# In the last group ScalarE shares the key search, and kept keys are marked behind it

## The chip, the cores and the metric

The kernel runs on one core of a Trainium2 chip. The metric is device time in microseconds (us) of one execution, lower is better. Engines: TensorE (PE, its weight loads PEld), VectorE (DVE), ScalarE (ACT), GpSimd (POOL) and SyncE (SP), which issues most DMAs.

## The reference

One decoder block on x of 2048 rows by 1024. A projection of the normed x gives a convolution branch, queries of 8 heads, one shared key and value head of 64, an indexer (8 small heads) and gates. For each row the indexer scores all earlier keys; the 256 highest are kept, and attention with ALiBi runs over the kept keys only. Then come the gated sum, a projection, a SwiGLU FFN of width 2816, and norms.

```python
rel = jax.nn.relu(jnp.einsum('bqhd,bsd->bqhs', qib, k_idx))
score = jnp.einsum('bqh,bqhs->bqs', wb, rel).astype(jnp.float32)
score = jnp.where(causal[None], score, -jnp.inf)
_, idx = lax.top_k(score, topk)          # topk = 256
...
x = x + merged @ w_out[layer]
hf = _rmsnorm(x, norm_ffn[layer])
x = x + (jax.nn.silu(hf @ w_ffn_gate[layer]) * (hf @ w_ffn_up[layer])) @ w_ffn_down[layer]
```

## The kernel before, in words

The rows are worked in four groups (g = 0 to 3) of 512, each of four row tiles of 128 (t = 0 to 3). The work has three kinds of stage: A (projection, convolution, gates, and at its end the indexer's scores), C (attention and output projection) and F (FFN). Their order is A0 C0, A1 F0 C1, A2 F1 C2, A3 F2 C3, F3: the FFN of a group runs behind the next group's A. Each engine has its own program, written out by hand in this order; semaphores tie them together.

*Key search* (L1143 to L1200, DVE, in stage A's program, but in time under the next F). SC holds each row's scores in f32, (4g + t + 1) * 128 of them for tile t; in group 3 these are 1664, 1792, 1920 and 2048. The search finds the 256th highest score bit by bit: in each of 31 turns of a loop (`one_bit`, L1165) DVE counts for each tile the scores at or above a candidate (L1151), then sets or leaves the bit (L1175 `change`, L1178 `cand`). A last count gives `room`, how many ties at the threshold may be kept (L1194).

*Marks* (`mark`, L948). For each unit of up to 512 keys four steps on DVE mark what is kept: L968 ties, L970 running rank of ties, L975 rank within room, L978 mark into SC (and a copy of the carry, L973). POOL turns marks into the mask M of distances (L505, L509). For groups 1 and 2 `marks_ahead` has tiles one to three (counted from 0) marked right behind the search; for groups 0 and 3 they are marked inside C, one unit in each of the first iterations of a row tile, between DVE's attention steps (L1226 to L1276): 12 units of up to 512 keys in C3. Tile 0 is always marked and masked by `first_mask` (L988), which DVE runs near the end of F.

*Stage F* (PE L1578 on, ACT L851 on, POOL L518 on). The 22 slices of the FFN's width go in parts of 8, 8 and 6. For each slice j of a part PE does a gate chunk into bank 6 and an up chunk into bank 7 (24 matmuls each); ACT applies Silu to the first (L873), copies the second (L878), POOL multiplies (L526), ACT and POOL split the product into high and low part (L864, L531). Then follow n row chunks (the down projection). PE may begin gate chunk j + 1 when Silu j is done, up chunk j + 1 when copy j is done. POOL adds earlier parts into XR (L539), and behind the last part's second down chunk writes the distances (`distances`, L472), which wait for `topk_done`, that is `room`. DVE's first mask waits for all additions to XR and for the distances.

*Border F to C.* DVE adds the last part into NY (L1327, four times); behind each of these ACT issues a DMA of two heads' queries (L907), and PE's first scores (L1555) wait for these.

*Stage C.* 16 pairs of heads (4 tiles x 4). For each head: PE scores in two parts, DVE adds the mask and takes the running minimum (L1251), ACT Exp (L809), PE transposes, ACT and DVE split them (L796, L1259), PE multiplies with the values; once per pair DVE takes a reciprocal (L1273).

The lines that set the order around the change:

```python
def marks_ahead(g):
    return 0 < g < GROUPS - 1
...
dve.wait_ge(y_added, 2 * RT * (len(PARTS) - 1) * (g + 1))
if g + 1 < GROUPS:
    first_mask(g + 1)
```

Of the kernel before, what the change touches and what calls it, by code (L numbers as in the profile page):

```python
# [23 lines left out]
def build_block(nc, A):  # L24
# [71 lines left out]
    def units(b):  # L96

        n = (b + 1) * P
        return [(s, min(512, n - s)) for s in range(0, n, 512)]

    IDX_UNITS = [sum(HEADS * len(units(b)) for b in blocks(g) if picks(b)) for g in range(GROUPS)]
    PICKED = [sum(picks(b) for b in blocks(g)) for g in range(GROUPS)]

# [17 lines left out]
    with ctx:  # L121
# [100 lines left out]
        idx_psum, idx_relu, idx_sum = sem("idx_psum"), sem("idx_relu"), sem("idx_sum")  # L222
        bit_step, topk_done, dist_ready = sem("bit_step"), sem("topk_done"), sem("dist_ready")
        mark_step, marked0, marked, m0_ready, m_ready, s_psum, s_masked, exp_done = sem("mark_step"), sem("first_keys_marked"), sem("keys_marked"), sem("first_mask_ready"), sem("mask_ready"), sem("s_psum"), sem("scores_masked"), sem("exp_done")
        pt_psum, pt_hi, pt_ready, pt_used = sem("pt_psum"), sem("pt_hi"), sem("pt_ready"), sem("pt_used")
# [88 lines left out]

        MASK_BASE = [sum((RT - 1) * (a + 1) for a in range(g)) for g in range(GROUPS)]

# [271 lines left out]
        def _(act):  # L588
# [53 lines left out]
            for ph, g in ORDER:  # L642
# [208 lines left out]
                else:  # L851
# [5 lines left out]
                    if g < GROUPS - 1:  # L857
                        act.wait_ge(idx_sum, sum(IDX_UNITS[:g + 2]))
                    for n in PARTS:
                        base_h = h_done  # L860
# [6 lines left out]
                        for j in range(n):  # L867
                            s = j % 2
                            used(c0 + 2 * j)
                            hi(c0 + 2 * j + 2, 0)  # L870
                            if j >= 2:
                                act.wait_ge(h_ready, base_h + j - 1)
                            nc.scalar.activation(TMP[:, s, :], PS[:, 6, :], ACT.Silu).then_inc(sg_done, 1)  # L873
                            if j >= 1:
                                h_hi_part(j - 1)
                            used(c0 + 2 * j + 1)
                            hi(c0 + 2 * j + 3, 1)
                            nc.scalar.activation(TMP[:, 2 + s, :], PS[:, 7, :], ACT.Copy).then_inc(up_done, 1)  # L878
                        c0 += 2 * n
                        h_done += n  # L880
                        for j in range(n - 1):
                            used(c0 + j)
                            hi(c0 + j + 2, (c0 + j) % 2)
                            if j == 0:
                                h_hi_part(n - 1)
                        if last_part:
                            hi(c0 + n + 1, 1)
# [27 lines left out]
        def _(dve):  # L915
# [32 lines left out]
            def mark(t, b, u, step):  # L948
# [33 lines left out]
                marks[0] += 1  # L982

            def marks_ahead(g):

                return 0 < g < GROUPS - 1

# [44 lines left out]
            for ph, g in ORDER:  # L1032
                c0 = BASE[ph, g]
                if ph == "A":
# [81 lines left out]
                    for t, b in enumerate(blocks(g)):  # L1116
# [23 lines left out]
                        dve.wait_ge(idx_sum, idx_done)  # L1140
                        chained(nc.vector.tensor_tensor(out=SC[:, t, n - P:n], in0=SC[:, t, n - P:n], in1=upper[:, :], op=ALU.add))


# [17 lines left out]
                    chained(nc.vector.tensor_scalar(flip[:, :], count[:, :], float(TOPK), -1.0, ALU.is_lt, ALU.mult))  # L1161
                    chained(nc.vector.tensor_tensor(out=cand[:, :], in0=trial[:, 0:1].to_broadcast([P, RT]), in1=flip[:, :], op=ALU.bitwise_xor))
                    TURNS = len(chosen) + 2

# [16 lines left out]

                    if g == 0:

# [4 lines left out]
                    else:  # L1188
                        with dve.Fori(0, 31) as i:
                            one_bit(i)  # L1190
                    turns[0] += 30 * TURNS

                    count_rows(ALU.is_gt, chained)
# [437 lines left out]
```

## Time and profile before

| | us |
|---|---|
| median of 3 runs | 3488.89 (3484.62 to 3489.68) |
| the profiled execution | 3484.34 |
| its span, first to last instruction | 3482.5 |
| PE busy | 3214.0 (92%) |
| DVE busy | 2176.4 (62%) |
| ACT busy | 1183.2 (34%) |
| POOL busy | 715.5 (21%) |
| mean granted TensorE clock, share of full speed | 0.975 |

The sums of the prediction are made on the profiled execution; its span leaves out 1.8 us around the instructions. Busy shares are means over stages with different limits, so the stages are read one by one. A timeline row gives start, duration, engine, line, operation, output <- inputs, count, and in brackets the engine's idle time before it and what ended that.

### The profile page before, as it was taken

Reading aid. Unit: us, or ns where it says so; the run is one execution under the profiler, and the core shown is the slowest. Engines: PE = TensorE matmul, PEld = TensorE weight load, DVE = VectorE, ACT = ScalarE, POOL = GpSimd, SP = SyncE. Lnnn points to the kernel's source line nnn. Section 1 sums busy time; section 2 is a strip of 40 time slices with the busy share of each in tenths; the row PEclk is TensorE's granted clock in tenths of the full one; section 3 lists DMA queues with packets and bytes.
Section 4 is the critical chain, followed back from the end, with each engine's and each line's share of the span. In section 5 each row is a group of like instructions: output and inputs, shape, how many; then the busy total and the mean of one; then the engine's idle time right before and its main releaser. Section 6 shows DMA issues by size and latency. Waiting matters only on the chain.

```text
span 3482.5 us, 41585 instructions
## 1 busy us (share of the span) xinstructions
PE 3214.0 (92%) x15045; PEld 2623.4 (75%) x15045; DVE 2176.4 (62%) x3647; ACT 1183.2 (34%) x2028; POOL 715.5 (21%) x482
## 2 busy tenths in 40 slices
PE   7991799999999999999999889999999968889998
PEld 6871688778887888768887778875888756768886
DVE  2758727588824827599894872759999988710001
ACT  3341541253335631261112753127111156521111
POOL 3430110035767000001214200000221231001212
PEclk9995899999999999999999999999999999999999
DMA  7970565569996366535555125652555510255554
GB/s 229 301 243 0 182 254 206 188 230 290 289 291 227 134 229 207 180 145 193 193 193 181 67 96 222 207 184 99 194 194 193 189 49 22 108 196 193 193 193 165
DMA packets 177613, 640.14 MB, mean 184 GB/s; under 512 B 11341, under 2 KB 95353, under 8 KB 115608
## 3 DMA queue, kind: packets, MB, share of 16 engines
q1 hardware_dynamic: 160800, 575.71, 48.0%
q10 hardware_dynamic: 16632, 61.96, 4.6%
q8 instruction: 121, 1.98, 0.2%
q14 instruction: 60, 0.49, 0.0%
HBM read 476.14 MB, written 161.48 MB: 183 GB/s over the span
## 4 chain that ended last, share of the span: by engine, by line
PE 64%; DVE 15%; issue 12%; ACT 5%; DMA 2%; POOL 1%; DVEq 0%; ACTq 0%; SPq 0%; POOLq 0%
PE PS L1391 14%; PE PS L1362 13%; PE PS L1364 13%; PE PS L1363 13%; DVE flags L1151 2%; PE PS L1510 2%; DVE probs L1251 2%; DVE W L1136 1%; PE PS L1376 1%; PE PS L1377 1%; PE PS L1378 1%; DMA RAW<-in_w_in 1%; ACT probs L809 1%; DVE PT L1259 1%; PE PS L1345 1%
## 5 line engine op out<-in xcount | busy, mean ns | idle before, releaser
L1151 DVE TENSOR_SCALAR_CACHE_REDUCE flags<-W,cand 128x1408 uint8<-128x1408 f32 (+3 forms) x462 | 683.5, 1479 | 53.8 <-DVE cand L1178 40.0
L1391 PE MATMUL PS<-WS,HT 128*128 128x512 f32 x2088 | 483.4, 391 | 5.1 <-POOL WS L455 2.8
L1391 PEld LDWEIGHTS PS<-WS,HT 128*128 128x128 f32 x2088 | 394.0, 189 | 88.5 <-issue 3.6
L526 POOL TENSOR_TENSOR TMP<-TMP 128x512 f32<-128x512 f32 x88 | 114.8, 1304 | 1538.8 <-ACT TMP L878 1538.8
L1362 PE MATMUL PS<-HF,WS 128*128 128x512 f32 x1072 | 417.4, 389 | 4.4 <-DVE HF L942 2.5
L1364 PE MATMUL PS<-HF,WS 128*128 128x512 f32 x1072 | 417.1, 389 | 0.0
L1363 PE MATMUL PS<-HF,WS 128*128 128x512 f32 x1072 | 417.1, 389 | 0.0
L455 POOL TENSOR_TENSOR WS<-RAW,WS 128x1024 fp32r<-128x1024 f32 x116 | 279.5, 2410 | 609.7 <-ACT WS L598 566.3
L1362 PE MATMUL PS<-HT,WS 128*128 128x512 f32 x824 | 325.2, 395 | 1.2 <-POOL WS L455 1.2
L1364 PE MATMUL PS<-HT,WS 128*128 128x512 f32 x824 | 320.8, 389 | 0.0
L1363 PE MATMUL PS<-HT,WS 128*128 128x512 f32 x824 | 320.6, 389 | 0.0
L1327 DVE TENSOR_TENSOR attn<-PS,XR 128x1024 f32<-128x1024 f32 x16 | 18.9, 1219 | 365.6 <-PE PS L1391 365.4
L1510 PE MATMUL PS<-ident,probs 128*128 128x128 f32 x1088 | 178.4, 286 | 70.9 <-ACT probs L809 28.6
L1362 PEld LDWEIGHTS PS<-HF,WS 128*128 128x128 f32 x1072 | 201.2, 188 | 47.5 <-issue 3.1
L598 ACT ACTIVATE WS<-RAW 128x1024 fp32r<-128x1024 f32 x114 | 120.8, 1059 | 335.3 <-PE PS L1364 151.5
L1364 PEld LDWEIGHTS PS<-HF,WS 128*128 128x128 f32 x1072 | 201.2, 188 | 41.7
L1363 PEld LDWEIGHTS PS<-HF,WS 128*128 128x128 f32 x1072 | 201.2, 188 | 41.7
L1016 DVE SCALAR_TENSOR_TENSOR PS<-W,cw,PS 128x512 f32<-128x512 f32 x336 | 221.9, 744 | 0.0
L1555 PE MATMUL PS<-KH,QS 128*128 128x512 f32 (+3 forms) x320 | 129.5, 405 | 99.8 <-DVE mx L1251 70.8
L1510 PEld LDWEIGHTS PS<-ident,probs 128*128 128x128 f32 x1088 | 128.6, 146 | 109.7 <-issue 60.7
L1391 PE MATMUL PS<-W,HT 128*128 128x512 f32 x792 | 184.9, 389 | 0.0
L1362 PEld LDWEIGHTS PS<-HT,WS 128*128 128x128 f32 x824 | 154.7, 188 | 35.6 <-issue 4.0
(219 smaller groups left out, 6039.0 us busy)
## 6 DMA issues: line engine op xcount, KB each, us to landing
WS<-split_weights_scratch SPq DMA_DIRECT2D x234, 1024.0 KB, 4.8
split_weights_scratch<-WS SPq DMA_DIRECT2D x116, 1024.0 KB, 5.0
W<-split_weights_scratch SPq DMA_DIRECT2D x114, 1024.0 KB, 4.8
RAW<-in_w_in SPq DMA_DIRECT2D x34, 512.0 KB, 6.1
RAW<-in_w_ffn_gate SPq DMA_DIRECT2D x22, 512.0 KB, 6.3
RAW<-in_w_ffn_up SPq DMA_DIRECT2D x22, 512.0 KB, 6.3
RAW<-in_w_ffn_down SPq DMA_DIRECT2D x22, 512.0 KB, 5.7
gate_b_scratch<-TMP ACTq DMA_DIRECT2D x32, 256.0 KB, 5.2
```

What stands on the lines that cost most here:

```text
L455: nc.gpsimd.tensor_tensor(out=WS[:, slot, 1, :], in0=RAW[:, slot, :], in1=WS[:, slot, 0, :].bitcast(f32), op=ALU.subtract).then_inc(w_lo, 1)
L526: nc.gpsimd.tensor_tensor(out=TMP[:, s, :], in0=TMP[:, s, :], in1=TMP[:, 2 + s, :], op=ALU.mult).then_inc(h_prod, 1)
L598: nc.scalar.activation(WS[:, slot, 0, :], RAW[:, slot, :], ACT.Copy).then_inc(w_hi, 1)
L1016: nc.vector.scalar_tensor_tensor(out=TAPSUM[:, c, :], in0=GLU[:, c, ds(k0 + i, ROWS)], scalar=cw[:, c, ds(k0 + i, 1)], in1=TAPSUM[:, c, :] ...
L1151: step(nc.vector.tensor_scalar(flags[:, 0:n], SC[:, t, 0:n], cand[:, t:t + 1].bitcast(f32), 0.0, op, ALU.add, accum_out=count[:, t:t + 1]))
L1251: nc.vector.tensor_tensor_reduce(out=prob(g, i, e)[:, s:s + w], in0=score_bank(r)[:, 0:w], in1=M[:, b % RT % 2, s:s + w].bitcast(f32), sca ...
L1362: mm(PS[:, bank, :], wh, src[:, 0, k, :], start=k == 0, stop=False)
L1363: mm(PS[:, bank, :], wh, src[:, 1, k, :], start=False, stop=False)
L1364: ins = mm(PS[:, bank, :], wl, src[:, 0, k, :], start=False, stop=k == KD - 1)
L1391: ins = mm(PS[:, 2 * t + half, :], lhs, split(c, w_part)[:, half * 512:(half + 1) * 512], start=first and part == 0 and w_part == 0, stop= ...
L1510: ins = nc.tensor.transpose(PS[:, 4 + k % 2, (2 * a + e) * P:(2 * a + e + 1) * P], prob(g, i, e)[:, (k0 + a) * P:(k0 + a + 1) * P], ident[ ...
L1555: mm(o, lhs, KH[:, s:s + w], start=True, stop=False)
```

## The change

Only group 3 is touched (`split_counts`). Its search loop runs on two engines: in each of the 31 turns DVE counts tiles 0 and 1 over 1792 scores (below the candidate), ACT tiles 2 and 3 over 2048 scores as a sum of signs of candidate minus score. The shorter rows are filled up to these lengths with the masked value. DVE waits for ACT's two sums, takes the bit step for all four tiles at once and posts the next trial. ACT's turns stand in F2's program: one behind each Silu (and high part) and one behind each up copy, none ahead of the first up copy, and one in each down chunk but the last two of a part; they stop at 31. ACT writes its signs into IH and IL, which nothing reads by then. A sum of signs can't tell ties at the candidate exactly, so `raise_by_one` behind the loop tries the next higher number for tiles 2 and 3. And `marks_ahead` now holds for group 3 too: the marks of row tiles two to four (t = 1 to 3) stand behind the search and no longer in C3.

```diff
--- before.py
+++ after.py
@@ -99,6 +99,11 @@
         return [(s, min(512, n - s)) for s in range(0, n, 512)]
 
     IDX_UNITS = [sum(HEADS * len(units(b)) for b in blocks(g) if picks(b)) for g in range(GROUPS)]
+    BITS = 31
+    SPLIT = RT // 2
+    COUNT_DVE, COUNT_ACT = SEQ - TOPK, SEQ
+
+
     PICKED = [sum(picks(b) for b in blocks(g)) for g in range(GROUPS)]
 
 
@@ -221,6 +226,7 @@
         qs_out, qs_in = sem("qs_out"), [sem(f"qs_in{t}") for t in range(RT)]
         idx_psum, idx_relu, idx_sum = sem("idx_psum"), sem("idx_relu"), sem("idx_sum")
         bit_step, topk_done, dist_ready = sem("bit_step"), sem("topk_done"), sem("dist_ready")
+        trial_ready, act_counted = sem("trial_ready"), sem("rows_counted_by_act")
         mark_step, marked0, marked, m0_ready, m_ready, s_psum, s_masked, exp_done = sem("mark_step"), sem("first_keys_marked"), sem("keys_marked"), sem("first_mask_ready"), sem("mask_ready"), sem("s_psum"), sem("scores_masked"), sem("exp_done")
         pt_psum, pt_hi, pt_ready, pt_used = sem("pt_psum"), sem("pt_hi"), sem("pt_ready"), sem("pt_used")
         rsb_ready, recip_done, pv_psum, bc_done, att_done = sem("rsb_ready"), sem("recip_done"), sem("pv_psum"), sem("bc_copied"), sem("att_done")
@@ -312,7 +318,7 @@
             return W3[:, part, :] if SLOT[c] == 2 else WS[:, SLOT[c], part, :]
 
 
-        MASK_BASE = [sum((RT - 1) * (a + 1) for a in range(g)) for g in range(GROUPS)]
+        MASK_BASE = [sum((RT - 1) * (a + 1) for a in range(g)) for g in range(GROUPS + 1)]
 
         def att_j(j):
             return att[:, j, 0:ROWS]
@@ -856,6 +862,19 @@
                     act.dma_start(XR[:, :, :], x1_dram[g]).then_inc(x1_in, 16)
                     if g < GROUPS - 1:
                         act.wait_ge(idx_sum, sum(IDX_UNITS[:g + 2]))
+                    turn = 0
+
+                    def count_rows():
+
+                        nonlocal turn
+                        if g + 2 != GROUPS or turn == BITS:
+                            return
+                        act.wait_ge(trial_ready, turn + 1)
+                        for t, seen in ((SPLIT, IH), (SPLIT + 1, IL)):
+                            nc.scalar.activation(seen[:, 0:COUNT_ACT], SC[:, t, 0:COUNT_ACT], ACT.Sign, scale=-1.0,
+                                                 bias=cand[:, t:t + 1].bitcast(f32), accum_out=count[:, t:t + 1]).then_inc(act_counted, 1)
+                        turn += 1
+
                     for n in PARTS:
                         base_h = h_done
 
@@ -873,9 +892,13 @@
                             nc.scalar.activation(TMP[:, s, :], PS[:, 6, :], ACT.Silu).then_inc(sg_done, 1)
                             if j >= 1:
                                 h_hi_part(j - 1)
+                            if j >= 1 or c0 > BASE[ph, g]:
+                                count_rows()
                             used(c0 + 2 * j + 1)
                             hi(c0 + 2 * j + 3, 1)
                             nc.scalar.activation(TMP[:, 2 + s, :], PS[:, 7, :], ACT.Copy).then_inc(up_done, 1)
+                            if j < n - 1:
+                                count_rows()
                         c0 += 2 * n
                         h_done += n
                         for j in range(n - 1):
@@ -883,6 +906,8 @@
                             hi(c0 + j + 2, (c0 + j) % 2)
                             if j == 0:
                                 h_hi_part(n - 1)
+                            if j < n - 2:
+                                count_rows()
                         if last_part:
                             hi(c0 + n + 1, 1)
                         if not last_part:
@@ -981,9 +1006,13 @@
                 ins.then_inc(mark_step, 1)
                 marks[0] += 1
 
+            def split_counts(g):
+
+                return g + 1 == GROUPS
+
             def marks_ahead(g):
 
-                return 0 < g < GROUPS - 1
+                return g > 0
 
             def first_mask(g):
 
@@ -1139,6 +1168,10 @@
                                 idx_done += 1
                         dve.wait_ge(idx_sum, idx_done)
                         chained(nc.vector.tensor_tensor(out=SC[:, t, n - P:n], in0=SC[:, t, n - P:n], in1=upper[:, :], op=ALU.add))
+                        if split_counts(g):
+                            to = COUNT_DVE if t < SPLIT else COUNT_ACT
+                            if n < to:
+                                chained(nc.vector.memset(SC[:, t, n:to], MASKED))
 
 
 
@@ -1159,8 +1192,13 @@
                     chained(nc.vector.memset(cand[:, :], 0))
                     count_rows(ALU.is_ge, chained)
                     chained(nc.vector.tensor_scalar(flip[:, :], count[:, :], float(TOPK), -1.0, ALU.is_lt, ALU.mult))
-                    chained(nc.vector.tensor_tensor(out=cand[:, :], in0=trial[:, 0:1].to_broadcast([P, RT]), in1=flip[:, :], op=ALU.bitwise_xor))
-                    TURNS = len(chosen) + 2
+                    ins = nc.vector.tensor_tensor(out=cand[:, :], in0=trial[:, 0:1].to_broadcast([P, RT]), in1=flip[:, :], op=ALU.bitwise_xor)
+                    if split_counts(g):
+                        ins.then_inc(trial_ready, 1)
+                        dve.wait_ge(trial_ready, 1)
+                    else:
+                        chained(ins)
+                    TURNS = 3 if split_counts(g) else len(chosen) + 2
 
                     def one_bit(i):
 
@@ -1179,7 +1217,52 @@
                                                             scalar=trial[:, ds(i + 1, 1)],
                                                             in1=cand[:, :], op0=ALU.bitwise_xor, op1=ALU.bitwise_xor))
 
-                    if g == 0:
+                    def one_bit_split(i):
+
+                        def turn(ins):
+
+                            ins.then_inc(bit_step, 1)
+                            turns[0] += 1
+                            dve.wait_ge(bit_step, turns[0] + TURNS * i)
+
+                        for t in range(SPLIT):
+                            turn(nc.vector.tensor_scalar(flags[:, 0:COUNT_DVE], SC[:, t, 0:COUNT_DVE], cand[:, t:t + 1].bitcast(f32), 0.0,
+                                                         ALU.is_lt, ALU.add, accum_out=count[:, t:t + 1]))
+
+                        dve.wait_ge(act_counted, 2 + 2 * i)
+                        turn(nc.vector.scalar_tensor_tensor(out=change[:, :], in0=count[:, :], scalar=float(COUNT_DVE - TOPK),
+                                                            in1=trial[:, ds(i, 1)].to_broadcast([P, RT]),
+                                                            op0=ALU.is_gt, op1=ALU.mult))
+                        nc.vector.scalar_tensor_tensor(out=cand[:, :], in0=change[:, :], scalar=trial[:, ds(i + 1, 1)],
+                                                       in1=cand[:, :], op0=ALU.bitwise_xor, op1=ALU.bitwise_xor).then_inc(trial_ready, 1)
+                        dve.wait_ge(trial_ready, 2 + i)
+
+                    def raise_by_one():
+
+                        found, turned = cand[:, SPLIT:RT], flip[:, SPLIT:RT]
+                        up, low, more = change[:, 0:2], change[:, 2:4], m8[:, 0:2].bitcast(i32)
+                        chained(nc.vector.tensor_tensor(out=up, in0=found, in1=turned, op=ALU.bitwise_xor))
+                        chained(nc.vector.tensor_scalar(low, up, 0xFFFF, None, ALU.bitwise_and))
+                        chained(nc.vector.tensor_scalar(low, low, 1.0, None, ALU.add))
+                        chained(nc.vector.tensor_scalar(up, up, 0x7FFF0000, None, ALU.bitwise_and))
+                        chained(nc.vector.tensor_scalar(more, low, 0x10000, None, ALU.bitwise_and))
+                        chained(nc.vector.tensor_tensor(out=up, in0=up, in1=more, op=ALU.add))
+                        chained(nc.vector.tensor_scalar(low, low, 0xFFFF, None, ALU.bitwise_and))
+                        chained(nc.vector.tensor_tensor(out=up, in0=up, in1=low, op=ALU.bitwise_or))
+                        chained(nc.vector.tensor_tensor(out=up, in0=up, in1=turned, op=ALU.bitwise_xor))
+                        for t in range(SPLIT, RT):
+                            n = (RT * g + t + 1) * P
+                            chained(nc.vector.tensor_scalar(flags[:, 0:n], SC[:, t, 0:n], change[:, t - SPLIT:t - SPLIT + 1].bitcast(f32), 0.0,
+                                                            ALU.is_ge, ALU.add, accum_out=count[:, t:t + 1]))
+                        chained(nc.vector.tensor_scalar(more, count[:, SPLIT:RT], float(TOPK), -1.0, ALU.is_ge, ALU.mult))
+                        chained(nc.vector.tensor_tensor(out=up, in0=up, in1=found, op=ALU.bitwise_xor))
+                        chained(nc.vector.tensor_tensor(out=up, in0=up, in1=more, op=ALU.bitwise_and))
+                        chained(nc.vector.tensor_tensor(out=found, in0=found, in1=up, op=ALU.bitwise_xor))
+
+                    if split_counts(g):
+                        with dve.Fori(0, BITS) as i:
+                            one_bit_split(i)
+                    elif g == 0:
 
                         start = turns[0]
                         for i in range(31):
@@ -1189,6 +1272,8 @@
                         with dve.Fori(0, 31) as i:
                             one_bit(i)
                     turns[0] += 30 * TURNS
+                    if split_counts(g):
+                        raise_by_one()
 
                     count_rows(ALU.is_gt, chained)
                     nc.vector.tensor_scalar(room[:, :], count[:, :], -1.0, float(TOPK), ALU.mult, ALU.add).then_inc(topk_done, 1)
```

## Rows read from the trace of the kernel before

**Rows 1.** Windows: stretch, its us, then busy us (instructions) of PE, PEld, DVE, ACT, POOL; PEclk

```profile
2423.00:2782.00 359.00, 359.00 (x1584) 297.18 (x1584) 331.45 (x359) 51.05 (x81) 77.32 (x61) 1.00 0.55 198
...
2785.00:2953.00 168.00, 126.22 (x802) 107.68 (x803) 147.32 (x273) 101.60 (x175) 43.84 (x39) 0.92 0.07 26
2953.00:3025.00 72.00, 61.60 (x430) 53.47 (x429) 57.19 (x107) 50.08 (x87) 1.16 (x1) 1.00 0.19 75
```

**Rows 2.** Timeline at the border F2 to C3: start, duration, engine, line, [idle before]

```profile
2767.29 0.17 DVE L1194 TENSOR_SCALAR room<-count 128x4 f32<-128x4 f32 x1
...
2785.42 4.61 DVE L1327 TENSOR_TENSOR attn<-PS,XR 128x1024 f32<-128x1024 f32 x4
2794.77 1.22 DVE L1251 CUSTOM_DVE_ANT_0 probs<-PS,QI 128x1024 f32<-128x1024 f32 x1 [4.75 <-PE PS L1556]
...
2757.01 1.28 POOL L539 TENSOR_TENSOR XR<-XR,YS 128x512 f32<-128x512 f32 x1
...
2768.07 1.29 POOL L539 TENSOR_TENSOR XR<-XR,YS 128x512 f32<-128x512 f32 x1
...
2777.74 4.47 PE L1391 MATMUL PS<-W,HT 128*128 128x512 f32 x19
2792.55 0.80 PE L1555 MATMUL PS<-KH,QS 128*128 128x512 f32 x1 [10.34 <-DMA QS<-q_scratch]
```

**Rows 3.** Timeline of DVE at the border F1 to C2

```profile
1893.83 2.36 DVE L1327 TENSOR_TENSOR attn<-PS,XR 128x1024 f32<-128x1024 f32 x2 [1.49 <-PE PS L1391]
1896.46 1.23 DVE L1251 CUSTOM_DVE_ANT_0 probs<-PS,QI 128x1024 f32<-128x1024 f32 x1 [0.28 <-PE PS L1556]
```

**Rows 4.** Groups by shape, whole span (busy us, mean ns | idle); a timeline row

```profile
L809 ACT ACTIVATE probs<-probs,mx 128x2048 f32<-128x2048 f32 x8 | 16.0, 2001 | 0.3 <-DVE mx L1251 0.3
...
L873 ACT ACTIVATE TMP<-PS 128x512 f32<-128x512 f32 x88 | 52.3, 594 | 308.1 <-PE PS L1364 308.1
...
L1151 DVE TENSOR_SCALAR_CACHE_REDUCE flags<-W,cand 128x1792 uint8<-128x1792 f32 x33 | 68.6, 2079 | 1.2
...
L1178 DVE SCALAR_TENSOR_TENSOR cand<-change,trial,cand 128x4 int32<-128x4 int32 x124 | 41.2, 333 | 15.2 <-DVE change L1175 10.8
...
2467.54 1.24 DVE L1175 SCALAR_TENSOR_TENSOR change<-count,trial 128x4 int32<-128x4 f32 x1
```

**Rows 5.** Groups of DVE's marks between 2785 and 2953 us

```profile
L970 DVE TENSOR_TENSOR_SCAN ties<-ties,carry 128x512 f16<-128x512 f16 (+2 forms) x9 | 10.7, 1185 | 0.0
L975 DVE SCALAR_TENSOR_TENSOR ties<-ties,room 128x512 f16<-128x512 f16 (+2 forms) x12 | 9.9, 824 | 0.3
L978 DVE SCALAR_TENSOR_TENSOR W<-W,cand,ties 128x512 f32<-128x512 f32 (+2 forms) x12 | 8.5, 710 | 0.0
L968 DVE TENSOR_SCALAR ties<-W,cand 128x512 f16<-128x512 f32 (+2 forms) x12 | 6.3, 524 | 0.0
...
L970 DVE TENSOR_TENSOR_SCAN ties<-ties 128x512 f16<-128x512 f16 x3 | 4.0, 1325 | 0.0
```

**Rows 6.** Timeline, reciprocals (L1273): first, eleventh, fifteenth of C3, then of C2

```profile
2810.86 0.16 DVE L1273 RECIPROCAL rs<-den 128x2 f32<-128x2 f32 x1
...
2952.13 0.16 DVE L1273 RECIPROCAL rs<-den 128x2 f32<-128x2 f32 x1
...
3003.16 0.16 DVE L1273 RECIPROCAL rs<-den 128x2 f32<-128x2 f32 x1
...
1906.91 0.16 DVE L1273 RECIPROCAL rs<-den 128x2 f32<-128x2 f32 x1
...
2000.98 0.17 DVE L1273 RECIPROCAL rs<-den 128x2 f32<-128x2 f32 x1
...
2041.68 0.17 DVE L1273 RECIPROCAL rs<-den 128x2 f32<-128x2 f32 x1
```

**Rows 7.** Groups of ACT over the whole span: a table load, and Square behind F's Silu

```profile
L873 ACT ACT_TABLE_LOAD x4 | 5.1, 1283 | 3.9 <-PE PS L1364 3.8
...
L910 ACT ACTIVATE TMP<-attn 128x1024 f32<-128x1024 f32 x16 | 16.9, 1058 | 92.1 <-DVE attn L1327 91.3 <-ACT TMP L910 0.3
```

## The prediction

> **What bounds the kernel now.** I read the views from the coarse to the fine. The busy time by stretch comes first [rows 1]. While FFN stage F2 runs (2423 to 2782 us), TensorE (PE) is busy for all of its 359.00 us: 66 weight chunks of 24 matmuls, so 5.44 us a chunk. VectorE (DVE) is busy for 331.45 us of it, nearly all of that group 3's key search, and ScalarE (ACT) for only 51.05 us. In attention stage C3 the bound is another: from 2785 to 2953 us, where DVE also marks the kept keys of row tiles two to four, DVE is busy for 147.32 of 168 us (88%), and from 2953 to 3025, without marks, for 57.19 of 72 us (79%). PE is at 75% and 86% there. So what bounds C3 is DVE's instructions together with the round trip DVE, ACT, PE, DVE of each head.
>
> Then the timeline at the border of F2 and C3 [rows 2]. The search ends with the write of `room` at 2767.29. POOL waits for that before it writes the distances, and its last addition to XR (L539) stands behind them: it starts only at 2768.07 and ends at 2769.36. DVE's first mask waits for this addition and takes 16.06 us, up to the adds into NY at 2785.42. PE finished F2 at 2782.21 (2777.74 + 4.47) and stands idle for 10.34 us, until the queries that ACT loads behind the first of these adds have landed (2792.55). DVE's first score reduction (L1251) starts at 2794.77. At the border of F1 and C2 nothing of this shows [rows 3]: there DVE waits for PE's last matmul (adds at 1893.83) and its first score reduction starts 2.63 us later, at 1896.46.
>
> **The change part by part.** (a) *The search itself.* Before, a turn of 31 is four counts of 1664 to 2048 keys and two small steps on DVE. Afterwards DVE counts two tiles of 1792 keys (2 x 2.08 us), and ACT two of 2048. The nearest row for ACT's Sign with a sum is Exp with a sum over the same 2048 f32 elements: 2.00 us [rows 4]; two with their read of the sum make 4.1 us. The bounds I keep are 1.8 and 2.4 us, the second being near DVE's time for such a count. The handshake of a turn is the change and cand steps and their semaphores: cand takes 0.33 us on the mean, change as much where POOL leaves it alone and 1.24 us where not [rows 4]; call it 0.8 us. So ACT can't turn faster than 4.1 + 0.8 = 4.9 us and DVE not faster than 4.3 + 0.8 = 5.1 us, and ACT's program lets only one turn go per chunk of PE: it goes at 5.44 us.
>
> Does ACT keep up? In a pair of column chunks (10.88 us) it has Silu, HT's high part and the up copy (3 x 0.6 us = 1.8 [rows 4]) and two turns (8.2 us): 10.0 us. The handshake passes beside the copies, all but about 0.2 us. That is 10.2 of 10.88 us: tight, but it fits. Silu has a whole chunk (5.44 us) to be late before PE waits. The new wait on ACT is for DVE's next trial; queued behind it stand Silu, HT's high part and the up copy, for which PE and POOL wait. At the start trial 1 comes some 4 us after ACT asks for it, and eats most of the slack; I take 0 us for it, with 0 to 3 us as bounds. DVE's new wait for ACT's counts holds up nothing but the search. In row chunks ACT has one turn of 4.1 us per 5.44 us and little else.
>
> The end of the search: part one of F2 holds 14 + 6 turns, so turn 21 falls behind chunk 25 and turn 31 behind chunk 35: 2423 + 35 x 5.44 = 2613 us, plus 6 us of Silu and count. `raise_by_one` (two counts, 13 small steps, some 8 us), the last count of four tiles (8.9 us) and the room step end near 2637 us instead of 2767.
>
> (b) *The marks* of tiles two to four move from C3 to behind the search. In C3 they cost DVE 10.7 + 9.9 + 8.5 + 6.3 + 4.0 = 39.4 us [rows 5]. Behind the search they cost as much and end near 2678 us. What hides them is DVE's idle time up to the first mask; it is gone if the search ends more than 80 us later than I reckon.
>
> (c) *The border F2 to C3.* POOL finds `room` long written, so its last addition follows the one at 2757.01 (ends 2758.3) and the distances (0.56 us): it ends near 2760. The first mask takes 16.06 us, to 2776. The first add into NY can start three quarters of a chunk before PE's end, at 2782.2 - 4.1 = 2778.1: the mask has 2 us in hand, and the border becomes that of F1 and C2. DVE's first score reduction then starts at 2782.2 + 2.6 = 2784.9 and not at 2794.77: **9.9 us** gained. ACT's DMAs of the queries move with the adds, one behind each; their landing time is the same. Beside the wait itself PE loses less speed: the granted clock of the marked stretch is 0.92 [rows 1] and the first matmuls behind the gap took 0.80 us. That lies under DVE's bound, and I count nothing for it.
>
> (d) *C3 without marks.* The reciprocal (L1273), one for each pair of heads, is the pulse of the stage [rows 6]. In C3, from the first to the eleventh it took 2952.13 - 2810.86 = 141.3 us, with marks. The next four intervals have none: 3003.16 - 2952.13 = 51.0 us. C2 is the same stage with 512 keys less in every row and already without marks: 94.1 us for the first ten intervals (1906.91 to 2000.98), 40.7 us for the next four (to 2041.68). So 512 keys more cost (51.0 - 40.7) / 4 = 2.6 us a pair, and C3 without marks would need 94.1 + 26 = 120 us: 21 us gained. That is a lower end, as C2's short rows wait more on round trips and would grow by less. The upper end: each interval's time less its marks (some 33 us of the 39 fall here), plus 0.5 us more of idle time a pair, as the unmarked stretch shows: 27 us gained. I take **24 us**, between these near ends. Ahead of the first reciprocal C3 took 2810.86 - 2794.77 = 16.1 us and C2 10.5 us; with 512 keys more in one and a half pairs this is 12 to 13: **3.5 us** gained (3 to 5).
>
> (e) *Small things.* Two memsets of 128 keys add 0.3 us ahead of the search, under PE's F2. POOL's masks and row scaling start 10 us earlier with the stage, and SP's waits for them (the stores of group 2's rows, the loads of GB and MA) with it: nothing waits there in C2's order, which is the same; 0 us. The tail from the last pair on, and F3, don't change.
>
> Sum: 9.9 + 24 + 3.5 = **37.4 us**. On the profiled execution (3484.34 us, span 3482.5) that is 3447. This execution lies 4.5 us under the median of the three runs, 3488.89; against the median it is **3451 us**. About 0.2% (7 us) is what a measurement of this kernel can tell from no change.
>
> **A rule against the change.** ACT changes between Silu and Sign twice a pair. Each function that is not in the loaded set needs a load of 1.28 us [rows 7]. The profile has such loads only ahead of Sigmoid, Silu, Sqrt and Exp; Copy, Relu and Square (L910, behind F's Silu) run under each set without one. Sign is as simple as these, so I count no load.
> The Trainium skill, "ScalarE: Activation LUTs", section "Table sets: the hidden batching unit", says that cheap functions are in every set but doesn't list Sign among them; its section on what a table load costs puts a switch at 2.66 us with its drain, of which the trace shows the 1.28 us. By that figure two switches a pair would cost 5.3 us.
>
> **The rivals.** *R1: table loads.* If Sign shares no set with Silu, a pair needs two loads: 10.2 + 2.6 = 12.8 us against PE's 10.88. PE then waits 1.9 us in each of the 11 pairs with two turns, some 21 us, less 5 us of slack: F2 16 us longer, 3467 us. For it: no row shows Sign. Against it: the simple functions above.
> *R2: slower.* The same place at a higher price: Sign's set lacks Copy too, and a pair has four loads, 10.2 + 5.1 = 15.3 us. PE waits 4.4 us a pair: 11 x 4.4 - 5 = 44 us lost in F2 against 37 gained, **3496 us**. It turns from gain to loss where a pair takes over 14.7 us, which counts of 3.1 us instead of 2.0 would do as well. Against it: Copy runs under every set in this trace.
> *R3: C3 is not bound by DVE's work but by the round trip.* Then a pair goes at the 13.0 us of the last unmarked intervals whatever is taken from DVE: ten intervals need 130 us, 11 gained, with 9.9 at the border and 2: 3466 us. Against it: C2's pairs go at 9 to 10.5 us with the same round trips.
> *R4: ACT keeps up only in part.* DVE's change step took 1.24 us where POOL works beside it [rows 4]; at two such steps a pair 10.2 becomes 12 us and PE loses 1.1 us in 11 pairs, less what slack is left: 10 us, 3461 us. For it: ACT is 94% full in these pairs. Against it: POOL's two short operations a pair mostly fall beside the counts.
> That the change doesn't do what it says is excluded by the diff, all but an ACT that computes the same counts.
>
> **How the numbers follow.** The sum as forecast 0.76; R4 0.08; R3 0.06; R1 0.06; R2 0.04. The likeliest case's own range: gains 24 + 3.5 + 9.9 with ends at 21, 3, 9 and 27, 5, 10.5, so 33 to 42.5 us, and a median that can lie 3 us off: 3443 to 3459. The range that holds 8 of 10 reaches up to R3 and R4: 3441 to 3465. Faster by over 0.2%: the forecast, R4, R3, R1 and some of the rest, 0.95; the same 0.02; slower 0.03.
>
> **What the profile will show.** F2 still 359 us with PE 100% busy and ACT at some 180 us; 62 Sign activations of about 2.0 us, turns 5.44 us apart, `room` written near 2637; marks behind it, then DVE idle until near 2760; PE's gap between F2 and C3 1.3 us instead of 10.3; reciprocals of C3 11 to 12 us apart for the first ten intervals; the last four unchanged. Table loads ahead of Silu and Sign in F2 would prove R1 or R2; idle PE in F2 without them R4; intervals at 13 us with DVE under 75% busy R3.

## The result, and the profile after

The changed kernel takes 3464.89 us (median, 3461.83 to 3466.2); the ratio to the kernel before is 0.9935, with a 95% interval from 0.992 to 0.9951. So it is some 24 us faster (23.7 between the medians, 22.7 by the ratio), where 37.4 were forecast. The median lies 0.1 us inside the upper end of the stated range (3465); by the ratio, 0.9935 x 3488.89 = 3466 us, it lies 1 us outside. A repetition beside the experiments gave 0.9934 (0.992 to 0.9947). The profiled execution took 3465.39 us, its span is 3463.6 us (3482.5 before).

The sum by parts, each from the two timelines:

| part | forecast | before | after | difference |
|---|---|---|---|---|
| F2, first to last matmul | 0 | 359.3 | 372.6 | **+13.2** |
| end of F2 to the first score reduction | -9.9 | 12.6 | 4.4 | -8.2 |
| from there to the first reciprocal | -3.5 | 16.1 | 12.1 | -4.0 |
| first to eleventh reciprocal | -24 | 141.3 | 115.1 | -26.2 |
| from there to the adds into XR | 0 | 131.4 | 131.7 | +0.3 |
| all ahead of F2 | 0 | 2422.9 | 2425.5 | +2.6 |
| from the adds into XR to the end | 0 | 399.0 | 402.2 | +3.2 |

I don't put the last two rows down to the change: the profiles below, whose code there is the same, begin F2 between 2418.2 and 2428.7 us and take 398.9 to 402.2 us from the adds into XR on. The three with 402.1 or 402.2 us (this one, its repetition and E6) show a granted clock of 0.94 from 3040 to 3200 us, the seven others, the kernel before among them, 0.96; why, no run shows. The other rows add up to -24.9 us. What is left is one surprise: TensorE's F2, the stage that was to pay nothing.

The border and the start of attention, timeline of the changed kernel (start, duration; answers to [rows 2]):

```profile
2653.45 0.30 DVE L1279 TENSOR_SCALAR room<-count 128x4 f32<-128x4 f32 x1
...
2774.65 1.29 POOL L545 TENSOR_TENSOR XR<-XR,YS 128x512 f32<-128x512 f32 x1
...
2775.97 0.48 DVE L993 TENSOR_SCALAR ties<-W,cand 128x512 f16<-128x512 f32 x1 [77.87 <-POOL XR L545]
...
2792.48 5.60 PE L1476 MATMUL PS<-W,HT 128*128 128x512 f32 x24
...
2800.69 0.50 PE L1640 MATMUL PS<-KH,QS 128*128 128x512 f32 x1 [2.61 <-DMA QS<-q_scratch]
...
2802.48 1.23 DVE L1336 CUSTOM_DVE_ANT_0 probs<-PS,QI 128x1024 f32<-128x1024 f32 x1 [2.01 <-PE PS L1641]
```

`room` is written at 2653 and not 2767, the marks follow it, VectorE (DVE) then idles 77.87 us until the last addition to XR, and TensorE (PE) waits 2.61 us for the queries where it had waited 10.34. The reciprocals of C3, first, eleventh and fifteenth (against [rows 6]):

```profile
2814.61 0.16 DVE L1358 RECIPROCAL rs<-den 128x2 f32<-128x2 f32 x1
...
2929.71 0.15 DVE L1358 RECIPROCAL rs<-den 128x2 f32<-128x2 f32 x1
...
2981.02 0.15 DVE L1358 RECIPROCAL rs<-den 128x2 f32<-128x2 f32 x1
```

The ten intervals shrank from 14.1 to 11.5 us on the mean; the four without marks stayed, 51.0 before and 51.3 after.

Now F2. What PE waited for between 2400 and 2800 us (us in total, times, longest):

```profile
PE PS L1476 <- ACT TMP L899: 3.1, 1, 3.1
PE PS L1447 <- ACT TMP L899: 3.1, 4, 0.8
PE PS L1447 <- ACT TMP L892: 2.8, 4, 0.7
```

Each time it was for ScalarE (ACT): for an up copy (L899) or a Silu (L892). These waits, 9.0 us in all, lie between 2469 and 2529 us, in the first of F2's three parts. Behind the longest (3.1 us, ahead of the part's first down chunk) the granted clock is down to 0.72 from 2528 to 2534 us, and matmuls take 0.63 us for 0.39. The three engines there:

```profile
2470.04 0.62 ACT L883 ACTIVATE HT<-TMP 128x512 fp32r<-128x512 f32 x1
2472.07 2.01 ACT L874 ACTIVATE IH<-W,cand 128x2048 fp32r<-128x2048 f32 x1 [1.42 <-DVE cand L1236]
...
2474.07 1.99 ACT L874 ACTIVATE IL<-W,cand 128x2048 fp32r<-128x2048 f32 x1
...
2476.06 0.58 ACT L899 ACTIVATE TMP<-PS 128x512 f32<-128x512 f32 x1
2478.50 2.01 ACT L874 ACTIVATE IH<-W,cand 128x2048 fp32r<-128x2048 f32 x1 [1.87 <-DVE cand L1236]
...
2470.68 1.35 DVE L1236 SCALAR_TENSOR_TENSOR cand<-change,trial,cand 128x4 int32<-128x4 int32 x1
...
2476.87 1.22 DVE L1233 SCALAR_TENSOR_TENSOR change<-count,trial 128x4 int32<-128x4 f32 x1 [0.23 <-DVE flags L1229]
...
2470.73 1.29 POOL L537 TENSOR_TENSOR HT<-TMP,HT 128x512 fp32r<-128x512 f32 x1 [5.59 <-ACT HT L883]
...
2476.78 1.30 POOL L532 TENSOR_TENSOR TMP<-TMP 128x512 f32<-128x512 f32 x1 [4.76 <-ACT TMP L899]
```

Read it as a circle. ACT ends its two signs at 2476.1 and at once does the up copy that is overdue. That releases GpSimd's (POOL) product at 2476.78. DVE's counts end at the same time, and its change step starts at 2476.87, 0.09 us behind POOL's operation. It should take 0.16 us and takes 1.22: it ends when POOL's operation ends. So the next trial comes 1.0 us late, ACT waits for it for 1.87 us, its copies are overdue again, and so on. In the turns before and behind this one it is the low part (L537) that meets the cand step (1.35 us for 0.22); the recorded start of that step, 2470.68, lies 0.05 us ahead of POOL's, 2470.73, and it too lasts until POOL's operation ends. Thirteen turns in a row, from 2451 to 2529 us, are hit in this way, and a turn takes 6.4 to 6.5 us where PE's chunk takes 5.44. Nor can DVE make up for a delay: without a meeting its turn takes 5.38 us, only 0.06 us less than a chunk.

### The profile page after: what moved, and what is told of

Same layout as the page of the kernel before. It is cut to its first block, busy times and chain, and to the rows that moved or that the text cites. A ratio compares the mean times of both kernels' runs of the same rounds, so it can differ in the third digit from the quotient of the medians.

```text
span 3463.6 us, 41578 instructions
## 1 busy us (share of the span) xinstructions
PE 3215.2 (93%) x15045; PEld 2625.7 (76%) x15045; DVE 2054.4 (59%) x3542; ACT 1306.6 (38%) x2152; POOL 714.7 (21%) x482
## 4 chain that ended last, share of the span: by engine, by line
PE 74%; DVE 12%; issue 6%; ACT 5%; DMA 2%; POOL 1%; DVEq 0%; ACTq 0%; SPq 0%; POOLq 0%
PE PS L1476 17%; PE PS L1447 15%; PE PS L1448 15%; PE PS L1449 15%; PE PS L1595 2%; DVE probs L1336 2%; DVE flags L1184 2%; PE PS L1461 1%; PE PS L1462 1%; PE PS L1463 1%; DVE W L1165 1%; ACT probs L815 1%; DVE PT L1344 1%; PE PS L1430 1%; ACT TMP L763 1%
## 5 line engine op out<-in xcount | busy, mean ns | idle before, releaser
L1184 DVE TENSOR_SCALAR_CACHE_REDUCE flags<-W,cand 128x384 uint8<-128x384 f32 (+6 forms) x338 | 417.4, 1235 | 37.9 <-DVE cand L1216 27.8
L1595 PE MATMUL PS<-ident,probs 128*128 128x128 f32 x1088 | 176.4, 284 | 51.3 <-ACT probs L815 32.4
L815 ACT ACTIVATE probs<-probs,mx 128x128 f32<-128x128 f32 (+15 forms) x128 | 153.3, 1198 | 75.4 <-DVE mx L1336 74.9
```

The lines of the kernel that those rows point to most:

```text
L815: nc.scalar.activation(row, row, ACT.Exp, bias=mx[:, i % held, e:e + 1], scale=-1.0, accum_out=den[:, i % held, e:e + 1]).then_inc(exp_don ...
L1184: step(nc.vector.tensor_scalar(flags[:, 0:n], SC[:, t, 0:n], cand[:, t:t + 1].bitcast(f32), 0.0, op, ALU.add, accum_out=count[:, t:t + 1]))
L1595: ins = nc.tensor.transpose(PS[:, 4 + k % 2, (2 * a + e) * P:(2 * a + e + 1) * P], prob(g, i, e)[:, (k0 + a) * P:(k0 + a + 1) * P], ident[ ...
```

## The experiments

Two theories stood: A, that this pace keeps itself up and only the late first trial starts it; B, that ACT and DVE simply can't do a turn in 5.44 us. All ratios are to the kernel before, run on the same chip.

**E1, the late first turn.**

```diff
-                            if j < n - 1:
+                            if j < n - 1 and (j > 0 or c0 > BASE[ph, g]):
                                 count_rows()
```

> Edit: ScalarE's first turn of the split search stands one slot later (behind the high part of slice 0, not behind the up copy of slice 0), so ScalarE no longer asks for the first trial 3.7 us before VectorE has it; nothing else changes. Theory A (a self-locking pace: the late start puts ScalarE's copies right behind its counts, they release GpSimd's operation in the very moment of VectorE's handshake, each handshake takes 1.0 us longer, and the delay keeps itself up at 6.45 us a turn): without the late start the turns of part one go at 5.44 us as in part two, TensorE loses nothing in F2 (359 us instead of 372), kernel about 3452 us, 13 us under the changed kernel. Theory B (ScalarE and VectorE can't do a turn in 5.44 us where there is also a high part to copy; part two only looks free because something else gives it time): the turns of part one stay near 6.4 us, TensorE still loses 9 to 13 us, kernel 3462 to 3466.

Measured: 3447.82 us, ratio 0.9894 (0.9877 to 0.991). F2 takes 359.3 us, and PE waits for ACT nowhere in it. B falls: both engines can do a turn in a chunk. For A it shows that the loss goes away with the late start; whether a delay keeps itself up is left to E7. E1's timeline of DVE and POOL in part one:

```profile
2476.91 0.17 DVE L1233 SCALAR_TENSOR_TENSOR change<-count,trial 128x4 int32<-128x4 f32 x1 [0.35 <-ACT IL L874]
2477.23 0.22 DVE L1236 SCALAR_TENSOR_TENSOR cand<-change,trial,cand 128x4 int32<-128x4 int32 x1 [0.15 <-DVE change L1233]
...
2467.00 1.30 POOL L532 TENSOR_TENSOR TMP<-TMP 128x512 f32<-128x512 f32 x1 [3.69 <-ACT TMP L899]
2472.89 1.31 POOL L537 TENSOR_TENSOR HT<-TMP,HT 128x512 fp32r<-128x512 f32 x1 [4.59 <-ACT HT L883]
```

ACT's copies are on time now, so they wait for PE's chunk and come behind the handshake; POOL's operations run beside DVE's counts, which they don't slow (2.08 us with or without). Turns take 5.37 to 5.51 us.

**E2, GpSimd yields.** The late start stays; in part one POOL's product of slice j waits for trial 2j + 1, its low part for trial 2j + 2.

```diff
+                        if g + 2 == GROUPS and c0 == BASE[ph, g] and j:
+                            pool.wait_ge(trial_ready, 2 * j + 1)
...
+                        if g + 2 == GROUPS and c0 == BASE[ph, g] and j < n - 1:
+                            pool.wait_ge(trial_ready, 2 * j + 2)
```

> Edit: in part one of F2 GpSimd's product and low part each wait until the next trial is posted, so they run beside VectorE's counts and not beside its two small handshake steps. The late start stays. Theory A' (it is the meeting of GpSimd's operation with the handshake that costs a turn 1.0 us): change and cand fall from 1.2 to 1.35 us to 0.16 and 0.22 us in every turn, a turn takes 5.4 us even with the late start, F2 about 360 to 362 us, kernel about 3453 us. Theory C (a turn is long because of its counts, and the handshake would wait for ScalarE anyway): the turn stays at 6.4 us, kernel 3465 or more, as GpSimd's operations now come later.

Measured: 3445.81 us, ratio 0.9893 (0.9877 to 0.991), F2 359.3 us. ACT's first turn of E2 is as late as ever, and POOL's operation now stands right behind the handshake:

```profile
2433.64 2.01 ACT L878 ACTIVATE IH<-W,cand 128x2048 fp32r<-128x2048 f32 x1 [3.71 <-DVE cand L1199]
...
2465.20 0.16 DVE L1237 SCALAR_TENSOR_TENSOR change<-count,trial 128x4 int32<-128x4 f32 x1 [0.23 <-DVE flags L1233]
2465.51 0.22 DVE L1240 SCALAR_TENSOR_TENSOR cand<-change,trial,cand 128x4 int32<-128x4 int32 x1 [0.15 <-DVE change L1237]
...
2465.91 1.30 POOL L534 TENSOR_TENSOR TMP<-TMP 128x512 f32<-128x512 f32 x1 [4.10 <-DVE cand L1240]
```

So the late start alone costs PE nothing: with the meeting taken away a turn takes 5.38 us. Theory C falls. More waits on POOL made the kernel 14 us faster (0.9934 against 0.9893).

**E6, both together.**

> Edit: the late first turn and the yielding GpSimd together (its waits shifted by the one turn). Theory A (both remove the same loss, the pace of part one): no more than either alone, F2 359.3 us, the same within 0.1% as the late start alone (about 36 us under the kernel before). If the two had removed different losses, it would be up to 13 us faster than either, which TensorE's 359 us in F2 exclude.

Measured: 3447.81 us, ratio 0.9897 (0.9882 to 0.9912), F2 359.3 us. Both remove one and the same loss.

**E7, one disturbance.** E1, and once, ahead of ACT's turn at slice 2, two copies of 2048 elements (E1's own edit and the line that makes the semaphore `bump` are left out here).

```diff
+                            if g + 2 == GROUPS and c0 == BASE[ph, g] and j == 2:
+                                act.wait_ge(act_counted, 2 * turn)
+                                for seen in (IH, IL):
+                                    nc.scalar.activation(seen[:, 0:COUNT_ACT], SC[:, SPLIT, 0:COUNT_ACT], ACT.Copy).then_inc(bump, 1)
+                                act.wait_ge(bump, 2)
```

> Edit: the late first turn (which goes at 5.44 us a turn), and on top of it one single disturbance: ahead of ScalarE's turn at slice 2 of part one two copies of 2048 elements (4.1 us) into the tiles that take the signs. Theory A (a delay keeps itself up by releasing GpSimd's operations into the handshake): from that slice to the end of part one each turn takes 6.4 us again, change and cand 1.2 us or more in turn, and TensorE loses 8 to 12 us in F2, not 4. Theory D (a delay is only passed on once): the turns behind it go at 5.4 us, TensorE loses 0 to 1 us, as 4.1 us is less than the chunk that a copy may be late.

Measured: 3457.83 us, ratio 0.9923 (0.9908 to 0.9938), so 10 us more than E1. F2 takes 367.4 us. The turn with the disturbance takes 9.2 us; two more go at 5.4; then, from the third on, they go at 6.42 to 6.51 to the end of the part, in seven turns of eight. PE's waits for ACT all lie at the end of it, from 2499 us on:

```profile
PE PS L1482 <- ACT TMP L905: 3.1, 1, 3.1
PE PS L1453 <- ACT TMP L905: 1.5, 2, 0.8
PE PS L1453 <- ACT TMP L893: 0.7, 1, 0.7
```

A single delay of 3.8 us, less than the 5.44 us that a copy may be late, cost PE 8.1 us. Theory A holds, D falls.

**E5, a handshake in nine steps with one input tensor each** (left out here: the tensor `above`, and one more semaphore step per turn).

```diff
-turn(nc.vector.scalar_tensor_tensor(out=change[:, :], in0=count[:, :], scalar=float(COUNT_DVE - TOPK),
-                                    in1=trial[:, ds(i, 1)].to_broadcast([P, RT]), op0=ALU.is_gt, op1=ALU.mult))
-nc.vector.scalar_tensor_tensor(out=cand[:, :], in0=change[:, :], scalar=trial[:, ds(i + 1, 1)],
-                               in1=cand[:, :], op0=ALU.bitwise_xor, op1=ALU.bitwise_xor).then_inc(trial_ready, 1)
+turn(nc.vector.tensor_scalar(above[:, :], count[:, :], float(COUNT_DVE - TOPK), -1.0, ALU.is_gt, ALU.mult))
+for t in range(RT):
+    ins = nc.vector.tensor_scalar(change[:, t:t + 1], above[:, t:t + 1], trial[:, ds(i, 1)], trial[:, ds(i + 1, 1)],
+                                  ALU.bitwise_and, ALU.bitwise_xor)
+turn(ins)
+for t in range(RT):
+    ins = nc.vector.tensor_scalar(cand[:, t:t + 1], change[:, t:t + 1], cand[:, t:t + 1], None, ALU.bitwise_xor)
+ins.then_inc(trial_ready, 1)
```

> Edit: the two steps of the handshake, each with two inputs in SBUF besides its scalar, are written as nine small ones with one input tensor each and [128, 1] scalars (compare; and, xor for each tile; xor for each tile). The late start stays, GpSimd doesn't yield. Theory E (what blocks is a VectorE instruction with two SBUF inputs while GpSimd reads SBUF): none of the nine takes over 0.3 us, also where GpSimd's operation runs; the handshake is some 1.2 us in every turn, turns take 5.6 to 5.9 us in part one and TensorE loses 2 to 5 us in F2, kernel 28 to 35 us under the one before. Theory F (any small VectorE instruction is held up while GpSimd works): some of the nine take over 1 us beside GpSimd, turns 6.8 us or more, TensorE loses over 15 us.

Measured: 3468.19 us, ratio 0.9962 (0.995 to 0.9974); F2 takes 381.9 us, turns of part one 6.52 to 6.55 us, but for two of 7.7 us. My size was wrong: nine steps take 1.9 us and not 1.2, so a turn is long without any meeting, and PE loses 22.6 us. What the run does tell is which instructions are held up. Groups of DVE (mean ns), and two turns of its timeline with POOL:

```profile
L1236 DVE TENSOR_SCALAR change<-above,trial 128x1 int32<-128x1 int32 x124 | 25.4, 268 | 5.6 <-DVE above L1234 5.6
L1234 DVE TENSOR_SCALAR above<-count 128x4 int32<-128x4 f32 x30 | 7.4, 246 | 9.7 <-ACT IL L875 5.9
```

```profile
2479.05 0.82 DVE L1236 TENSOR_SCALAR change<-above,trial 128x1 int32<-128x1 int32 x4 [0.18 <-DVE above L1234]
...
2485.23 1.31 DVE L1234 TENSOR_SCALAR above<-count 128x4 int32<-128x4 f32 x1
...
2479.15 1.29 POOL L538 TENSOR_TENSOR HT<-TMP,HT 128x512 fp32r<-128x512 f32 x1 [5.66 <-ACT HT L884]
...
2485.22 1.30 POOL L533 TENSOR_TENSOR TMP<-TMP 128x512 f32<-128x512 f32 x1 [4.78 <-ACT TMP L900]
```

The and-xor steps on one column ran beside POOL's operation turn after turn and took 0.82 us for four every time. The compare on four columns, with one input tensor, was held up twice (1.31 and 1.30 us for 0.17), both times where it started 0.01 us behind POOL's operation; ten more times the two started within 0.005 us of each other, and it wasn't. So both theories were too simple. E is wrong in that one input tensor doesn't protect; F in that not every small instruction is held up. The Trainium skill, "SBUF — State Buffer", section "Who interferes with whom", gives a rule that fits both: an instruction of VectorE contends with GpSimd if it has two SBUF inputs and GpSimd's instruction reads SBUF, or if it runs in a mode with two ports; the one that starts first keeps the shared ports to its end, and the other blocks fully. The single-input compare would be of the second kind; that the mode is the reason, no run here shows.

**The changed kernel again**, beside these runs.

> The changed kernel unchanged, for a comparison on the same chip as the others: 0.9935 of the kernel before, F2 at 370 to 373 us, turns of part one at 6.45 us.

Measured: 3459.86 us, ratio 0.9934 (0.992 to 0.9947); F2 takes 370.0 us, a turn of part one 6.41 to 6.50 us. So the loss is there again, 2.6 us smaller than in the first profile. The traces show why: here one cand step escapes,

```profile
2518.78 0.22 DVE L1236 SCALAR_TENSOR_TENSOR cand<-change,trial,cand 128x4 int32<-128x4 int32 x1 [0.15 <-DVE change L1233]
...
2518.83 1.34 POOL L537 TENSOR_TENSOR HT<-TMP,HT 128x512 fp32r<-128x512 f32 x1 [5.59 <-ACT HT L883]
```

so that 12 turns are hit and not 13 (as in E3, whose F2 takes 370.0 us too), PE's last wait is 2.0 us and not 3.1, and the granted clock stays at 1.00 behind it.

**E3 and E4, the two halves of the change alone.** E3 splits the search and leaves the marks in C3 (the first edit below); E4 leaves the search on DVE and moves the marks (the second, and ACT's turns are left out).

```diff
             def marks_ahead(g):
-                return g > 0
+                return 0 < g < GROUPS - 1
...
             def split_counts(g):
-                return g + 1 == GROUPS
+                return False
```

> Edit: the search is split as in the changed kernel, but the marks of row tiles two to four stay in C3 as before. By the sum of parts as the traces show it: F2 13 us longer, the border F2 to C3 8 us shorter, C3 as before: about 3493 us, 5 us over the kernel before. If instead the split brings something to C3 itself (warmer clock, masks earlier) it is under 3489.

> Edit: the search stays on VectorE alone as before, but the marks of row tiles two to four stand behind it and not in C3. The search ends at 2767, marks (40 us) at 2807, first mask (16 us) at 2823, adds into NY and first score reduction near 2833: the border costs 38 us more than before, C3 about 30 us less: about 3497 us, 8 us slower than before. If the marks in C3 had cost less than 30 us it is slower still; if TensorE's clock falls in the 45 us gap, by some us more.

Measured: E3 3490.29 us, ratio 1.0014 (1.0004 to 1.0023), E4 3497.33 us, ratio 1.0033 (1.0021 to 1.0046). First score reduction and adds into XR, E3 and then E4:

```profile
2802.91 1.23 DVE L1336 CUSTOM_DVE_ANT_0 probs<-PS,QI 128x1024 f32<-128x1024 f32 x1 [1.97 <-PE PS L1641]
...
3092.52 1.22 DVE L1395 TENSOR_TENSOR XR<-PS,XR 128x1024 f32<-128x1024 f32 x1 [34.77 <-PE PS L1476]
```

```profile
2837.94 1.23 DVE L1336 CUSTOM_DVE_ANT_0 probs<-PS,QI 128x1024 f32<-128x1024 f32 x1 [4.59 <-PE PS L1641]
...
3096.97 1.23 DVE L1395 TENSOR_TENSOR XR<-PS,XR 128x1024 f32<-128x1024 f32 x1 [34.77 <-PE PS L1476]
```

E3: 289.6 us between the two, as before (288.7), and F2 at 370.0 us: the split alone has the loss in F2 (10.7 us) and the shorter border (8.2 us), and comes out 5 us slower by the ratio. That is 0.14%, less than the 0.2% that the prediction took as the least that can be told, and it rests on the meeting: the split with E1's later start but without the moved marks was not run. E4: 259.0 us between them, as in the changed kernel (258.9), but the first score comes 53.5 us behind F2's end instead of 12.6. So neither half alone is a gain; the marks bring 30 us in C3, but only with a search that ends early enough to hide them.

## Why the prediction was right and wrong

**Right: C3 without marks.** Forecast 24 + 3.5 us, measured 26.2 + 4.0, and E4 shows the same 30 us with the search left as it was. The two terms together came out 2.7 us better than forecast. The estimate from the busy time, DVE's instructions less the marks plus some more idle time (27 us; its own terms, 33 less 5, give 28), was nearer than that from C2's pulse (21 us). Rival R3 (the round trip bounds C3) is out.

**Right in kind: the border.** 8.2 us instead of 9.9. PE waited 2.6 us for the queries, where C2 had let me expect 1.3. The step that was off is that the queries land as at C2's border: from the issue of the first of their DMAs to PE's first score matmul it took 5.3 us here (2795.37 to 2800.69) and 4.0 us there (1891.09 to 1895.12). The other 0.4 us are PE's first score matmuls, most of them 0.63 us here and 0.40 there; the granted clock was 0.77 from 2798 to 2804 us and 1.00 at C2's border.

**Right: the table loads.** No load stands ahead of a Sign; F2 has a single one, ahead of its first Silu as before. R1 and R2 are out. Sign takes 2.01 us for 2048 elements, as the Exp row said.

**Wrong: "tight, but it fits".** The step that failed is the one that took F2's cost as 0 (bounds 0 to 3 us). It measured 13.2 us (10.7 in E3, and 10.7 us in the repetition). That both engines can do a turn in a chunk was right, if tighter than in the sum: E1 and E2 keep PE at 359.3 us, with a free turn of DVE at 5.38 us where the sum had 5.1. What failed is the handshake's price of 0.8 us in every turn. I had the row of a change step of 1.24 us beside a working POOL [rows 4], and gave it to rival R4 at 8%, since POOL's operations "mostly fall beside the counts". That held for ACT on time. It didn't ask where they fall once ACT is late: ACT's own overdue copies release them, and so they fall exactly on the handshake. The slack of 5.44 us that I counted as cover for the late start was eaten at 1.0 us a turn. R4 had the right meeting, and its 3461 us is near what came in part by luck: a pair took 12.9 us and not 12, but PE waited in part one alone and not in 11 pairs.

The trace before could have warned me, for that row was no single case. In 13 of the 31 turns of the search there (five in part one, four in each other part) the change step takes 1.24 to 1.25 us, each time 0.05 to 0.07 us behind a POOL operation. Two of them, DVE and then POOL:

```profile
2478.41 1.25 DVE L1175 SCALAR_TENSOR_TENSOR change<-count,trial 128x4 int32<-128x4 f32 x1
...
2489.29 1.25 DVE L1175 SCALAR_TENSOR_TENSOR change<-count,trial 128x4 int32<-128x4 f32 x1
...
2478.35 1.28 POOL L526 TENSOR_TENSOR TMP<-TMP 128x512 f32<-128x512 f32 x1 [3.69 <-ACT TMP L878]
...
2489.23 1.28 POOL L526 TENSOR_TENSOR TMP<-TMP 128x512 f32<-128x512 f32 x1 [3.70 <-ACT TMP L878]
```

Their starts lie 10.88 us apart, two chunks of PE, where a free turn of that search takes 9.79 us. So the meeting repeated from turn to turn already there, only that nothing waited for the search.

The end of the search, 2653 instead of 2637 us: 2.6 us are F2's later start and 8 us the same loss (counted from F2's first matmul `room` is written after 227.9 us, in E1 after 219.7); the other 6 us were undercounted. It cost nothing, with 80 us of cover. Against the likeliest case of the prediction, then, E1 is the kernel that it described: forecast 37.4 us under the kernel before, measured 36.5 us. That these are so near is in part luck: E1's border gained 7.5 us and not 9.9, and its C3 28.9 us and not 27.5.

The version to keep is E1 (one condition more) or E2: 1.06% and 1.07% faster than the kernel before, where the change as made brings 0.65%. Between the two nothing can be told apart. What stays open is why the queries take 5.3 us at this border.

## What to carry to other kernels

When two engines pass a small step to and fro inside a pace set by a third, cost the step once with everything on time and once with one engine late, and ask what the late engine's overdue work releases, and which small step that will meet: slack that covers a delay once doesn't cover a delay that renews itself. Starting a turn later, or letting the engine that has time wait for the handshake, can be worth more than any shorter instruction. And look in the trace before whether a lengthened step comes again at the same distance behind another engine's operation: then it is a pattern and not a chance. Where a change has two halves, run each alone: here neither half was a gain, and the two together were.

## What the runs showed of the hardware that was not expected

- DVE's change and cand steps on [128, 4] that meet a POOL tensor_tensor on [128, 512] last until 0.02 to 0.03 us behind its end: 1.19 to 1.36 us for 0.16 and 0.22 where their recorded start lies between 0.05 us ahead of POOL's and 0.12 behind it, and still 1.09, 0.63 and 0.32 us where it lies 0.21, 0.68 and 1.00 us behind it (kernel before). The profile shows this as a longer step and not as idle time. Steps on [128, 1] beside the same operation are not held up (0.82 us for four in every turn of E5), nor is the count over 1792 elements with its sum (2.08 us).
- It hangs on thousandths of a microsecond who is first. In E5 the compare took 0.17 us ten times (five in part one: 2446.04, 2459.12, 2472.17, 2499.43 and 2512.48) where its recorded start is between 0.001 us ahead of that of POOL's product and 0.005 us behind it, and the product took 1.32 or 1.33 us there; in the two turns where it started 0.009 and 0.010 us behind it took 1.3 us, and the product 1.28 and 1.30. A cand step whose recorded start lay 0.047 to 0.049 us ahead of POOL's low part was not held in four cases (repetition, E3, twice in E7), and the low part took 1.34 us; at 0.046 us ahead or less it was held each time.
- An added wait on POOL, in the middle of PE's busiest stage, took 14 us off the kernel.
